# Copies of kept state rows issued by ScalarE on its hardware DMA queue in place of GpSimd on the software queue

## What is computed

```python
A_GROUPS = ((128, 1), (512, 4), (2048, 16))
...
for g, (window, dil) in enumerate(A_GROUPS):
    buf = win_states[g]
    n_buf = buf.shape[1]
    kv_all = jnp.concatenate([buf, jnp.stack([ka[:, :, g], va[:, :, g]], axis=2)], axis=1)
    o, lse = _dilated_sample(qa[:, :, g], kv_all[:, :, 0], kv_all[:, :, 1], n_buf, window, dil, slopes[g])
    ...
    win_new.append(kv_all[:, T:])
```

## Time and profile before

| | |
|---|---|
| median of 3 runs | 4280.96 us (4279.13 to 4285.91) |
| profiled execution, its own time | 4272.16 us |
| its span | 4270.6 us |
| busy share PE, PEld, DVE, ACT, POOL | 82%, 69%, 32%, 22%, 9% |
| dilated stage in the span | about 137 to 1478 us |
| q0, q1, q10: MB moved | 152.99, 247.53, 4.20 |
| PE clock granted, mean | 0.874 |

### The profile page before, as it was taken

The page is one execution under the profiler, slowest core; times in us unless marked ns, Lnnn a source line. Parts: engine busy times, 40 slices in busy tenths (PEclk is TensorE's granted clock), DMA queues, the critical chain, the costliest instruction groups (busy, mean ns, idle before and its releaser), DMA issues. The chain is left out here.

```text
span 4270.6 us, 56660 instructions
## 1 busy us (share of the span) xinstructions
PE 3504.9 (82%) x19368; PEld 2959.0 (69%) x19368; DVE 1369.5 (32%) x3897; ACT 939.5 (22%) x1791; POOL 377.9 (9%) x498
## 2 busy tenths in 40 slices
PE   7899999999999999999799999924444665318989
PEld 7777777777788799999576677714443665318967
DVE  5132222222222311000455555512221222483333
ACT  5222222222222211111344444400000111001022
POOL 0000000000000000000000000012222333002300
PEclk9999999999999799999899999965555667659999
DMA  4333333332333121221100000035552222465443
GB/s 134 127 107 100 108 110 111 111 104 80 97 97 105 51 75 60 74 74 55 50 13 11 12 12 12 10 124 182 189 186 64 60 55 62 164 220 197 160 134 117
DMA packets 311967, 407.54 MB, mean 95 GB/s; under 512 B 73129, under 2 KB 269578, under 8 KB 306778
## 3 DMA queue, kind: packets, MB, share of 16 engines
q1 hardware_dynamic: 278714, 247.53, 19.3%
q0 software_dynamic: 23824, 152.99, 10.3%
q10 hardware_dynamic: 9216, 4.20, 0.3%
HBM read 317.41 MB, written 175.28 MB: 115 GB/s over the span
## 5 line engine op out<-in xcount | busy, mean ns | idle before, releaser
L109 PE MATMUL dil_J<-all_xT_hi,dil_w_hi 128*128 128x512 f32 x1152 | 473.7, 411 | 14.6 <-DVE dil_w_lo L714 12.1
L111 PE MATMUL dil_J<-all_xT_hi,dil_w_lo 128*128 128x512 f32 x1152 | 455.1, 395 | 0.0
L110 PE MATMUL dil_J<-all_xT_lo,dil_w_hi 128*128 128x512 f32 x1152 | 454.6, 395 | 0.0
L109 PE MATMUL gate_ps<-all_xT_hi,gate_w_hi 128*128 128x416 f32 x960 | 338.4, 352 | 9.1 <-DVE gate_w_lo L969 9.1
L110 PE MATMUL gate_ps<-all_xT_lo,gate_w_hi 128*128 128x416 f32 x960 | 336.9, 351 | 0.0
L111 PE MATMUL gate_ps<-all_xT_hi,gate_w_lo 128*128 128x416 f32 x960 | 336.6, 351 | 0.0
L1251 PE MATMUL mla_S<-mla_k,mla_q 96*128 96x512 f32 (+3 forms) x640 | 279.0, 553 | 15.7 <-ACT mla_p L1138 8.9
L739 DVE CUSTOM_DVE_ANT_0 dil_sm<-dil_S,dil_bias 128x256 f32<-128x256 f32 (+1 forms) x384 | 125.0, 363 | 498.6 <-PE dil_S L831 427.5
L1279 PE MATMUL mla_O<-mla_v,mla_pT 128*128 128x66 f32 x2176 | 264.6, 271 | 2.6 <-DVE mla_pT L1198 1.7
L109 PEld LDWEIGHTS dil_J<-all_xT_hi,dil_w_hi 128*128 128x128 f32 x1152 | 217.7, 189 | 68.7 <-issue 14.2
L685 ACT ACTIVATE dil_sm<-dil_sm,dil_neg 128x256 f32<-128x256 f32 (+1 forms) x384 | 156.6, 455 | 483.4 <-DVE dil_neg L745 483.4
(11 more groups left out here) (262 smaller groups left out, 6063.0 us busy)
## 6 DMA issues: line engine op xcount, KB each, us to landing
out_win_sample<-in_state_win POOLq DMA_DIRECT2D x8, 8128.0 KB, 27.0
sdil_kv<-in_state_win SPq DMA_DIRECT2D x72, 512.0 KB
scr_gates<-gate_out POOLq DMA_DIRECT2D x24, 1040.0 KB, 4.5
sdil_qb<-scr_hs SPq DMA_DIRECT2D x32, 768.0 KB
dil_raw<-in_w_in SPq DMA_DIRECT2D x36, 512.0 KB, 4.0
proj_gm<-scr_gates SPq DMA_DIRECT2D x40, 416.0 KB, 3.3
out_win_sample<-in_state_win POOLq DMA_DIRECT2D x8, 1984.0 KB, 11.3
scr_oa<-dil_rec SPq DMA_DIRECT2D x192, 66.0 KB, 1.6
```

What stands on the lines that cost most here:

```text
L109: pe.matmul(out, w[0], x[0], start=first, stop=False)
L110: pe.matmul(out, w[0], x[1], start=False, stop=False)
L111: return pe.matmul(out, w[1], x[0], start=False, stop=last)
```

## The change

The function `move` goes from POOL's program to ACT's and issues with `act.dma_start`, which uses q10. It is called in tick 2 of each section from 0 to 11, behind `values_staged` and ahead of `empty_turned`, once for the group 2 copies in sections 0 to 7 and for groups 1 and 0 in sections 8 to 11. POOL's waits for `vT_ready` go; the DMAs on ACT have no wait of their own.

```diff
-                for b in range(DB):
-                    pool.wait_ge(vT_ready, b * 4 + 1)
-                    move(2, b, b + 1)
-                for b in range(0, DB, 2):
-                    pool.wait_ge(vT_ready, (b // 2 + DB) * 4 + 1)
-                    move(1, b, b + 2)
-                    move(0, b, b + 2)
...
             def _(act):
+                def move(g, first, last):
...
+                    for b in range(first, last):
+                        act.dma_start(new[b, 0:whole, :].rearrange("(s i) n -> s i n", s=16),
+                                       old[b, DT:DT + whole, :].rearrange("(s i) n -> s i n", s=16))\
+                            .then_inc(copied, 16)
+                    act.dma_start(new[first:last, whole:kept, :], old[first:last, DT + whole:DT + kept, :])\
+                        .then_inc(copied, 16)
...
                             if 2 <= tick <= 8:
                                 values_staged(s, tick // 2 - 1)
+                            if tick == 2 and s < DB:
+                                move(2, s, s + 1)
+                            elif tick == 2:
+                                move(1, 2 * (s - DB), 2 * (s - DB) + 2)
+                                move(0, 2 * (s - DB), 2 * (s - DB) + 2)
```

More of the change, by code:

```diff
@@ L647, in _ @@
             def _(act):
+                def move(g, first, last):
+                    kept = GROUPS[g][0] - DT
+                    whole = kept // 16 * 16
+                    new = t[f"win{g}_sample"].rearrange("b i c n -> b i (c n)")
+                    old = t[f"state_win{g}"].rearrange("b i c n -> b i (c n)")
+                    for b in range(first, last):
[4 more added lines that the diff above has]
+                        .then_inc(copied, 16)
                 def high(i):
```

## The result

The changed kernel takes 4304.0 us (median of 7 runs, 4292.8 to 4312.9), against 4281.0 (median of 7) for the kernel before: ratio 1.0049, 95% interval 1.003 to 1.0068. The profiled execution took 4295.8 us, 23.6 more than that of before.

The account below looks back on a forecast made before the run. PE bounds the dilated stage, losing 19.3 us waiting for DVE's mask, whose release follows the copy's start. Idle time 16.4 + clock 9.6 = +26 us on 4272.2, plus 9 to the median: 4307 us; range 4265 to 4337 at 0.8.

Parts of the forecast that it names:

- The chain: Dilated stage: copy's start sets its end, then q1's load and records land, DVE's mask follows, PE's wait ends; 29.85 us in section 2.
- no change: Rival: the copy on q10 ends when it did on q0, 1.8 to 2.35 us shorter; 4281 us, chance 0.15.
- about 36: Sign that the forecast is right: PE's wait for DVE's mask in the dilated stage grows from 19.3 to about 36 us.
- The issue's place: ACT's DMA leaves right behind the waiting exponential of tick 1, ahead of the staged values' start: 1.55 us after POOL's in section 2.
- late issue: Rival: the DMA leaves only behind the staged values on ACT's engine; 4329 to 4338 us, chance 0.07.
- issue ahead: Rival: ACT issues ahead of its waiting instruction; same time as the faster rival, 4249 us, no chance of its own given.
- Idle time: PE's added waits for the mask from the later copies: 7.2 us in sections 1 to 4, 7.05 in 5 to 7, 2.2 in 9 to 11.
- The 2.2 us of sections 9 to 11: PE's added wait there: a shift of 1.6 us less 0.87 us to spare, 0.73 in each of three sections.
- The clock: Sections 5 to 7 drop to the 1.2 GHz level behind PE's idle time: 3 x 3.2 = 9.6 us, or 0 if it holds.
- ACT's issue cost: One DMA issue takes ACT's sequencer 349 ns, 2.1 us for six in sections 8 to 11; covered by queued work, costed at nothing.
- Faster, finer turns: Rival: smaller packets on q10 or more turns for SP's queue end PE's wait and four clock spells; 4249 us, chance 0.17.
- ACT held: Rival: ACT is held in the issue for a whole copy, 27 us, once it no longer fits the queue; 4395 us, chance 0.05.

Follow-up runs that it names:

- experiment 1: The kernel before with eight record buffers in place of six in the dilated stage: 4248.2 us, ratio 0.9916.
- experiment 2: The changed kernel with eight record buffers in place of six: 4250.3 us, ratio 0.9919 to the kernel before.
- experiment 3: The kernel before, copies still on POOL's q0, but POOL also waits for the negated maximum that releases ACT's exponential of tick 1: 4311.8 us, ratio 1.0061.
- 7: The changed kernel with each of the eight long copies in two halves, ten ticks apart: 4246.4 us, ratio 0.9927 to the kernel before.
- experiment 6: The kernel before with only the small copies of each section's last rows issued by ACT, the bulk copies left on POOL: 4272.6 us, ratio 0.9991.
- 4: The changed kernel with ACT issuing each section's copies in tick 0 in place of tick 2: 4249.7 us, ratio 0.9915 to the kernel before.
- 5: The kernel before, copies still on POOL but released two ticks earlier, by the last query projection of the section before: 4242.7 us, ratio 0.9921.
- 8: The changed kernel with each long copy as two copies in pieces of one 2 KB row: 4365.0 us, ratio 1.0207 to the kernel before.
- experiment 9: The kernel before, copies on POOL, with each long copy as two copies in pieces of one 2 KB row: 4263.5 us, ratio 0.9966.

## Why the prediction was right, step by step

**The chain held.** The distance from issue to mask stayed at 29 to 30 us in section 2, on q10 as on q0; q10 and q1 took turns, one packet each, so the rival "no change", a copy shorter by 1.8 us or more on q10, has nothing for it. The wait of 33.8 us stands against "about 36". Experiments 1 and 2 show that the record ring carries the loss, 3 that the moment of issue does, 7 that the copy's end does.

**The issue's place held.** ACT's sequencer passed the staged values and not the waiting exponential; of the rivals "late issue" would have had the DMA at 344.73 + 0.57 = 345.30, and "issue ahead" before 342.97. The later start is 1.57 us in section 2, where 1.55 had been forecast, 2.15 in section 5, as forecast (scores of tick 1 at 678.47 and 687.79, issues at 678.84 and 690.31), and 1.70 in section 9, where it was 1.4 (1138.41 and 1157.06, 1138.78 and 1159.13). Of the 0.2 us added for the first packets on q10, 0.1 is in the means of experiment 3.

**Idle time: 14.5 of the forecast 16.4 us.** In sections 1 to 4 PE's waits grew by 7.5 us (7.2 forecast; 1.4 in section 2 to 2.45 in section 1), in 5 to 7 by 7.0 (7.05 forecast). **The 2.2 us of sections 9 to 11 did not come.** In section 9 DVE's wait grew by 6.25 - 5.22 = 1.03 us, not 1.6: the issue came 1.70 us later, but the distance from there to the mask was 1181.73 - 1159.13 = 22.60, against 23.29 before. PE, with the narrower blocks of that group, can go on 0.57 us behind the mask (1282.39 and 1282.96 in section 10), not the 0.84 taken from section 2. So it had 1.71 - 0.57 = 1.14 us to spare, and the 1.03 fit in.

**The clock: the term that was mis-sized.** That sections 5 to 7 would drop was right, the 9.6 us were not. Their spells are shorter than in section 2: over the 6.7 us behind each wait the clock reads 0.75, 0.56 and 0.75, a loss of 6.7 x 0.25 = 1.7, 3.0 and 1.7 us at most, 6.4 in all. Over the whole stage, the longer spells of sections 1 to 4 included (0.63 over 10.3 us in section 2 costs 3.8 us at most, against 3.2 before), it is less: from first to last score PE's busy time over the same 6756 instructions grew by 1225.85 - 1220.58 = 5.3 us (stretches, before and after). The 3.2 us for a spell, too, were more than the 2.83 that experiment 1 gives for section 2.

```profile
221.60:1464.30 1242.70, 1220.58 (x6756) 962.96 (x6755) 355.11 (x1536) 307.96 (x663) 18.91 (x38) 0.98 0.32 100
...
222.20:1483.10 1260.90, 1225.85 (x6756) 968.05 (x6755) 354.98 (x1536) 307.95 (x663) 0.00 (x0) 0.97 0.31 98
```

The idle time in these rows grew by 35.05 - 22.12 = 12.9 us. The waits for the mask grew by 14.5, while PE's waits for ACT's staged values, which the forecast had not touched, fell by 1.7, from 2.3 us in four waits to 0.6 in one (view of waits, before and after, the stage alone):

```profile
PE dil_J L109 <- ACT dil_kT L663: 2.3, 4, 0.6
...
PE dil_J L109 <- ACT dil_kT L655: 0.6, 1, 0.6
```

So the stage came 7.8 us short of the 26: 1.9 of waits for the mask, 1.6 of other idle time, 4.3 of clock. That the median is short by 3 us only is luck: the profiled execution lost another 5 us outside this stage, which no step of the forecast had, and the interval of the ratio, 13 to 29 us, would hold the 18.2 of the stage as well.

**ACT's issue cost: too low, without effect.** An issue took 0.54 us (bulk) and 0.62 us (tails) in the median and up to 1.13, not the 0.35 taken from another copy's row. In section 2 ACT's engine had work queued until 345.30. In sections 8 to 11, with six issues, the cover that the forecast counted on was too short, and the engine stood idle behind them, 8.0 us in four times (view of waits):

```profile
ACT dil_pT L649 <- issue: 8.0, 4, 2.3
```

"Costed at nothing" stood all the same: with eight buffers, experiments 1 and 2, the stage takes 1214.0 us without ACT's issues and 1213.9 with them, and experiment 6 found no cost.

**The rivals.** "Faster, finer turns" had the right price for a wait that goes, 4249 (experiments 1, 2, 4, 5 and 7 lie within 7 us of it), but the copy's packets on q10 were the 65 KB of q0. Smaller packets, experiments 8 and 9, took the wait to 0.6 and 5.3 us and neither kernel to that price. The rule cited for it, 9 to 17 descriptors a turn (the Trainium skill, "DMA: Bandwidth & Descriptors", "Queues, rings and completion order"), is not what the rows show for two hardware queues either, if a packet of the profile is a descriptor: 16 against 16. "ACT held" does exist, but not with 8 or 9 pieces per engine; it came with 127 per DMA and engine (4064 KB in rows of 2 KB, on 16 engines), two such DMAs in a row and a third behind them.

## To carry to other kernels

A transfer that nobody waits for can still sit on the critical path, through what shares its DMA engines: look for the wait that ends a fixed time behind its issue, and move the start, halve the transfer, or give the ring behind it two more buffers, before asking which engine should issue it. When a DMA moves to an engine with an instruction stream of its own, what costs is the waiting instruction ahead of it there, so put the DMA in front of that, here for 0.8%. Here a few packets of 65 KB held up those of another queue on the same DMA engines, and many of 2 KB held ACT, which issued them.

## What was not expected of the hardware

The issue on ACT took 0.54 to 0.62 us in the median for copies between two places in device memory, against 0.35 us for its loads of 64 KB into the chip. Idle time of 2.0 us in section 4 of experiment 9 left the clock at its full level, as 1.78 did, while 3.3 to 3.9 us in sections 5 to 7 of the changed kernel did not. How long the low spell lasts does not follow the idle time: 3.89, 3.43 and 3.33 us were followed by 0.75, 0.56 and 0.75 over 6.7 us. The stretch behind those 2.0 us:

```profile
577.80:584.50 6.70, 6.41 (x52) 5.29 (x52) 2.06 (x11) 2.46 (x6) 0.00 (x0) 1.00 0.16 53
```

The stages behind this one differ from profile to profile by nearly as much as this change is worth: experiment 2 has the scores of experiment 1 to 0.1 us and a span of 4261.0 against 4245.7 us. Over half of this is busy time of PE over the same 11616 instructions behind the last score (2115.3 and 2123.7 us), the rest idle time; what makes them differ was not tried.
